# The start of a two-block transformer kernel: first weights loaded piece by piece between the halves of x, squares of x summed on GpSimd, rounded parts of two pieces ahead of the rests

## What is computed

```python
def rmsnorm(x, g):
    xf = x.astype(jnp.float32)
    y = xf * lax.rsqrt(jnp.mean(xf * xf, axis=-1, keepdims=True) + EPS)
    return (y * g.astype(jnp.float32)).astype(x.dtype)
...
        h = rmsnorm(x, g_mix[i])
        z = h @ w_in[i]                                   # 1024 x 2560
        b_gate, c_gate, x_in, u, v = jnp.split(z, splits, axis=-1)
        y_conv = short_conv_mixer(b_gate, c_gate, x_in, w_conv[i])
        y_sgu = sgu_mixer(jax.nn.gelu(u), jax.nn.gelu(v), g_sgu[i], w_spatial[i], b_spatial[i])
        x = x + jnp.concatenate([y_conv, y_sgu], axis=-1) @ w_out[i]
```

## Time and profile before

| | |
|---|---|
| time, median of 3 runs | 951.76 us (950.13 to 953.07) |
| the profiled execution's span | 949.0 us |
| median less that span | 2.76 us |
| TensorE busy | 921.4 us, 97% |
| TensorE weight loads (beside the products) | 650.6 us, 69% |
| VectorE / ScalarE / GpSimd busy | 501.4 / 330.9 / 36.0 us |
| read from HBM | 287.43 MB, 304 GB/s over the span |

### The profile page before, as it was taken

The page is one execution under the profiler, slowest core; times in us unless marked ns, Lnnn a source line. Parts: engine busy times, 40 slices in busy tenths (PEclk is TensorE's granted clock), DMA queues, the critical chain, the costliest instruction groups (busy, mean ns, idle before and its releaser), DMA issues.

```text
span 949.0 us, 14172 instructions
## 1 busy us (share of the span) xinstructions
PE 921.4 (97%) x5886; PEld 650.6 (69%) x5886; DVE 501.4 (53%) x867; ACT 330.9 (35%) x528; POOL 36.0 (4%) x39
## 2 busy tenths in 40 slices
PE   7999999999999899999999999999999999999997
PEld 6997734443444445334344389989999999999886
DVE  7784612221222312222222199999898977766642
ACT  6832210101011000001101088556566755644541
POOL 1000000000000000000000000123220000000000
PEclk9999999999999999999999999999999999999999
DMA  9997799999999999999999984643433435554301
GB/s 334 407 388 311 302 387 430 424 431 430 430 430 432 428 427 431 429 430 430 430 430 422 422 357 177 246 163 126 168 134 144 178 111 194 227 202 178 134 1 44
DMA packets 28981, 289.45 MB, mean 305 GB/s; under 512 B 3056, under 2 KB 6384, under 8 KB 12400
## 3 DMA queue, kind: packets, MB, share of 16 engines
q1 hardware_dynamic: 28192, 286.91, 74.0%
q10 hardware_dynamic: 720, 1.57, 0.4%
HBM read 287.43 MB, written 1.05 MB: 304 GB/s over the span
## 4 chain that ended last, share of the span: by engine, by line
PE 86%; DVE 8%; ACT 3%; issue 2%; DMA 0%; DVEq 0%; POOL 0%; ACTq 0%
PE ps L279 85%; DVE wl L275 3%; PE ps L1081 1%; ACT wh L268 1%; DMA arena<-in_xT 0%; ACT arena L1903 0%; DVE arena L393 0%; DVE arena L1944 0%; DVE arena L2015 0%; DVE ple_l L1477 0%; ACT h_h L1449 0%; DVE arena L1486 0%; DVE mg_l L1951 0%; ACT arena L1906 0%; DVE mix_l L624 0%
## 5 line engine op out<-in xcount | busy, mean ns | idle before, releaser
L279 PE MATMUL ps<-ring,arena 128*64 128x512 f32 x1216 | 340.2, 600 | 5.9 <-issue 5.9
L275 DVE TENSOR_TENSOR wl<-ring,wh 128x1024 fp32r<-128x1024 f32 x150 | 181.5, 1243 | 40.2 <-ACT wh L268 40.1
L279 PEld LDWEIGHTS ps<-ring,arena 128*64 128x64 f32 x1216 | 109.1, 138 | 125.0 <-issue 123.2
L268 ACT ACTIVATE wh<-ring 128x1024 fp32r<-128x1024 f32 x150 | 151.9, 1053 | 43.2 <-PE ps L279 30.4
L279 PE MATMUL ps<-arena 128*64 128x512 f32 (+4 forms) x448 | 158.4, 522 | 0.5 <-DVE arena L1173 0.3
L1186 DVE SCALAR_TENSOR_TENSOR arena<-ps,arena 128x512 f32<-128x512 f32 x16 | 12.0, 752 | 205.0 <-PE ps L279 205.0
L279 PEld LDWEIGHTS ps<-arena 128*64 128x64 f32 (+2 forms) x448 | 54.7, 144 | 86.6 <-issue 82.1
L279 PE MATMUL ps<-up_h,wh 128*128 128x256 f32 x352 | 85.7, 282 | 0.7 <-ACT up_h L2004 0.7
L279 PE MATMUL ps<-up_l,wh 128*128 128x256 f32 x352 | 82.3, 280 | 0.0
L1256 ACT ACTIVATE y_h<-ps 128x512 fp32r<-128x512 f32 x32 | 19.0, 597 | 151.7 <-PE ps L279 151.7
L279 PEld LDWEIGHTS ps<-up_h,wh 128*128 128x128 f32 x352 | 66.3, 188 | 0.9 <-issue 0.9
(11 more groups left out here) (279 smaller groups left out, 1466.3 us busy)
## 6 DMA issues: line engine op xcount, KB each, us to landing
ring<-in_moe SPq DMA_DIRECT2D x69, 2048.0 KB, 23.6
arena<-in_moe SPq DMA_DIRECT2D x17, 2048.0 KB, 23.6
ring<-in_w_in SPq DMA_DIRECT2D x12, 2048.0 KB, 9.7
ring<-in_w_up SPq DMA_DIRECT2D x11, 2048.0 KB, 7.6
ring<-in_moe SPq DMA_DIRECT2D x24, 512.0 KB, 15.3
ring<-in_w_dn SPq DMA_DIRECT2D x5, 2048.0 KB, 8.1
ring<-in_w_out SPq DMA_DIRECT2D x4, 2048.0 KB, 16.1
arena<-in_moe SPq DMA_DIRECT2D x8, 512.0 KB, 13.9
```

Source lines behind the costliest of these rows:

```text
L268: e.activation(wh(i), raw_piece(i), ACT.Copy).then_inc(*hi.up(i))
L275: e.tensor_tensor(wl(i), raw_piece(i), wh(i), SUB).then_inc(*lo.up(i))
L279: return e.matmul(o, l, r, start=first, stop=final, skip_group_check=True)
```

## The change

- The host lays the first load out by pieces, so that each piece is 4 KB in one stretch per partition, where it was eight stretches of 512 bytes.
- SyncE's order becomes: first half of x, gains, piece 0, second half of x, piece 1, pieces 2 and 3 together, and the rest as before.
- All eight squares are made by GpSimd, which then adds them up itself: chunks 4 to 7 onto 0 to 3 (128 x 1024 values), 2 and 3 onto 0 and 1 (512), 1 onto 0 (256). TensorE multiplies the one sum, after piece 2, where it multiplied eight squares ahead of piece 0.
- TensorE begins with seven float32 products of ones into an unused bank, which wait for nothing but memsets; then piece 0's products with x's rounded parts and rests for chunks 0 to 3 and for 4 to 7, then piece 1's, then the rests of pieces 0 and 1, piece 2, the sum's product, piece 3.
- ScalarE makes piece 0's rounded part between the halves of x, and pieces 1 to 5 before the root r1 (before: 0 to 3). VectorE makes the rests of pieces 0 to 5 before the reciprocal (before: 0 to 3).

```diff
@@ mixer_pe
-            squares((1, 0, 3, 2, 5, 7, 4, 6))
-            three(e, ps[3][:, 0:256], "in1", 0, 0, XGH, XGL, xg)
-            for j in range(1, 4):
-                three(e, ps[3 + j][:, 0:256], "in1", 0, j, XGH, XGL)
+            for x in range(7):
+                mm(e, ps[7][:, 0:256], inv1024, ones[:, 0:2, :].rearrange("p a b -> p (a b)"), x == 0, x == 6)
+            e.wait_ge(*hi.at(0))
+            products(0, range(4), wh, xg_h)
+            products(0, range(4), wh, xg)
+            products(0, range(4, 8), wh, xg_h)
+            products(0, range(4, 8), wh, xg)
+            e.wait_ge(*hi.at(1))
+            products(1, range(8), wh, xg_h)
+            products(1, range(8), wh, xg)
+            rounded_rest(0)
+            rounded_rest(1)
+            three(e, ps[5][:, 0:256], "in1", 0, 2, XGH, XGL)
+            e.wait_ge(*sum0.at("all"))
+            mm(e, ps[2][:, 0:256], inv1024, SQ0[:, 0, :], True, True).then_inc(*means.up("r1"))
+            three(e, ps[6][:, 0:256], "in1", 0, 3, XGH, XGL)
@@ mixer_dve
-                if c in (0, 2):
-                    e.tensor_tensor(SQ0[:, c, :], XT[:, c, :], XT[:, c, :], M).then_inc(*sq0_v.up(c))
-                    e.wait_ge(*sq0_v.at(c))
-                elif c in (4, 6):
-                    e.wait_ge(*sq0_a.at(c))
-                else:
-                    e.wait_ge(*sq0_p.at(c))
+                e.wait_ge(*sq0.at(c))
...
-            split_lo(e, 4)
+            split_lo(e, 6)
@@ mixer_act
             for c in range(8):
+                if c == 4:
+                    split_hi(e, 1)
...
-                if c in (4, 6):
-                    e.activation(SQ0[:, c, :], XT[:, c, :], ACT.Square).then_inc(*sq0_a.up(c))
-            split_hi(e, 4)
+            split_hi(e, 6)
@@ mixer_pool
-            for c in range(1, 8, 2):
+            for c in range(8):
                 e.wait_ge(l_xT if c < 4 else l_xT2, 16)
-                e.tensor_tensor(SQ0[:, c, :], XT[:, c, :], XT[:, c, :], M).then_inc(*sq0_p.up(c))
+                e.tensor_tensor(SQ0[:, c, :], XT[:, c, :], XT[:, c, :], M).then_inc(*sq0.up(c))
+            e.wait_ge(*sq0.at(7))
+            e.tensor_tensor(SQ0[:, 0:4, :], SQ0[:, 0:4, :], SQ0[:, 4:8, :], ADD).then_inc(*sum0.up("four"))
+            e.wait_ge(*sum0.at("four"))
+            e.tensor_tensor(SQ0[:, 0:2, :], SQ0[:, 0:2, :], SQ0[:, 2:4, :], ADD).then_inc(*sum0.up("two"))
+            e.wait_ge(*sum0.at("two"))
+            e.tensor_tensor(SQ0[:, 0, :], SQ0[:, 0, :], SQ0[:, 1, :], ADD).then_inc(*sum0.up("all"))
@@ loads
-            e.dma_start(XT[:, 4:8, :], dr["xT"][:, 4:8, :]).then_inc(l_xT2, 16)
...
-                    dst, src = (v.rearrange("p (c n) -> p c n", c=8) for v in (dst, src))
-                    e.dma_start(dst[:, :, 0:128], src[:, :, 0:128]).then_inc(ring_sem[k], 16)
-                    e.dma_start(dst[:, :, 128:256], src[:, :, 128:256]).then_inc(l_second, 16)
-                    e.dma_start(dst[:, :, 256:512], src[:, :, 256:512]).then_inc(s_half, 16)
+                    e.dma_start(dst[:, 0:1024], src[:, 0:1024]).then_inc(ring_sem[k], 16)
+                    e.dma_start(XT[:, 4:8, :], dr["xT"][:, 4:8, :]).then_inc(l_xT2, 16)
+                    e.dma_start(dst[:, 1024:2048], src[:, 1024:2048]).then_inc(l_second, 16)
+                    e.dma_start(dst[:, 2048:4096], src[:, 2048:4096]).then_inc(s_half, 16)
@@ _layout
+    r["w_in"][0] = r["w_in"][0].reshape(128, 8, 4, 128).transpose(0, 2, 1, 3).reshape(128, -1)
```

More of the change, by code:

```diff
@@ L216, in raw_piece @@
                 return w[:, j * 1024:j * 1024 + 1024]
-            if name == "pgate":
+            if name == "pgate" or (name, n) == ("in1", 0):
                 return piece_view(w[:, j * 1024:j * 1024 + 1024], name)
@@ L428, in build @@
         xg_h = sig("x_hi", range(8))
-        sq0_v, sq0_a, sq0_p = sig("sq0_v", [0, 2]), sig("squares", [4, 6]), sig("sq0_p", range(1, 8, 2))
+        sq0 = sig("sq0", range(8))
+        sum0 = sig("sum0", ["four", "two", "all"])
         xg = sig("x_lo", range(8))
@@ L475, in mixer_pe, with products, rounded_rest @@
         def mixer_pe(e):
-            def squares(cs):
+            def products(j, cs, v, ready=None):
                 for c in cs:
[L478 to L481, removed]
-            e.wait_ge(*made.at("ones"))
-            squares((1, 0, 3, 2, 5, 7, 4, 6))
-            three(e, ps[3][:, 0:256], "in1", 0, 0, XGH, XGL, xg)
-            for j in range(1, 4):
-                three(e, ps[3 + j][:, 0:256], "in1", 0, j, XGH, XGL)
+                    if ready is not None:
+                        e.wait_ge(*ready.at(c))
+                    k = mm(e, ps[3 + j][:, 0:256], v(j)[:, c, :], (XGL if ready is xg else XGH)[:, c, :],
+                           v is wh and ready is not xg and c == 0, v is wl and c == 7)
+                return k
+            def rounded_rest(j):
+                e.wait_ge(*lo.at(j))
+                products(j, range(8), wl).then_inc(*proj.up("in1", 0, j))
+            e.wait_ge(*made.at("ones"))
+            for x in range(7):
[14 more added lines that the diff above has]
+            three(e, ps[6][:, 0:256], "in1", 0, 3, XGH, XGL)
             for i in range(2):
@@ L651, in build @@
         xc = sig("xc", range(2))
-        vsq = sq0_a.then(range(2))
+        vsq = sig("squares", range(2))
         vvar = sig("vvar", [0])
```

## The result

The changed kernel takes 955.79 us (median of 5 runs, 954.78 to 957.18) against 951.02 us for the kernel before beside it: a ratio of 1.0055, 95% interval 1.0044 to 1.0067, so 5.2 us slower (4.2 to 6.4). The profiled execution took 956.97 us and has a span of 955.2 us, which leaves 1.8 us around the span.

What follows compares the result with a forecast made beforehand. TensorE was taken to bound the start, transfers from 138 to 328 us. Turns with GpSimd's additions (4.0 us) put piece 3's end at 26.4, half clock (0.6) at 27.0; 3.4 us late after VectorE's last rest: 951.76 + 3.4 = 955.2, range 950.9 to 956.8.

Steps and rivals of the forecast that it cites:

- a shift at the start reaches the end one for one: Each us TensorE wins or loses at 27 us counts as one us at the end, in either direction.
- second mark: Start of TensorE's first product with rests of pieces 4 to 7: forecast 30.75 against 27.35 before, 3.4 us late.
- x's second half at 9.5: In the first transfers, x's second half lands behind piece 0 at 9.5 us, 1.4 us later than before.
- Rival (d): The layout fails and x's second half comes at 10.5: one us more in every case, 956.2 us; chance 0.05.
- The pairs of square and rest: GpSimd's squares and VectorE's rests of x alternate: after square 4, three pairs of 0.82 us each, to 12.65.
- The long addition goes first: GpSimd's addition of 1024 columns runs ahead of VectorE's rest of chunk 7, from 12.65 to 14.9, 2.25 us.
- Who goes first: When both want to run, waiting GpSimd goes before the next VectorE operation; likely, with the other order kept as rival.
- (b): VectorE makes chunk 7's rest first, additions slip between pieces' rests: 0.9 to 2.1 us slower, 953.4 us; chance 0.22.
- (c): VectorE wins every meeting and TensorE waits for the late sum: 3.8 us slower with half clock, 955.6; chance 0.10.
- (a): VectorE and GpSimd don't hinder each other where it counts: 0.35 us faster, 951.4 us; chance 0.13.
- The clock: TensorE runs 3.3 us after 15.2 at half clock: 0.6 us lost after hiding by a wait, bounds 0 and 1.9.
- first mark: Start of TensorE's first product with 512 columns, where piece 3 ends: forecast 27.0 against 23.60 before.

Runs made afterwards that it cites:

- e10: Changed kernel without additions, squares on three engines as before, their products where TensorE waits for x, pieces 4 and 5 behind root and reciprocal: 949.51 us, ratio 0.9993.
- e3: Changed kernel with the rounded parts and rests of pieces 4 and 5 put back behind the root and the reciprocal: 957.28 us, ratio 1.0073.
- e8: Kernel before with the new layout of the first load and seven products of ones ahead of the squares' products, x's second half still ahead of piece 0: 949.61 us, ratio 0.9983.
- e2: Changed kernel with nine more products of ones, so that TensorE doesn't stand idle before 15.2 us: 953.8 us, ratio 1.0043.
- e1: Changed kernel with GpSimd's three additions left out, TensorE multiplying the square of chunk 0 alone: 952.59 us, ratio 1.0016.
- e4: Kernel before with only the new layout of the first load and the new order of its transfers: 952.26 us, ratio 1.0017.
- e7: Kernel before with only the seven products of ones put ahead of the squares' products: 949.72 us, ratio 0.9989.
- e6: Kernel before with GpSimd's squares and additions, seven products of ones and the one late product; transfers, layout and orders as before: 957.63 us, ratio 1.007.
- e5: Changed kernel with one more wait: GpSimd begins its additions only when the rest of x's chunk 7 is made: 953.16 us, ratio 1.0023.
- e9: e5 with five more products of ones to keep TensorE's clock up: 954.4 us, ratio 1.0037.

## Why the prediction was right

The forecast was 955.2 us and 3.4 us slower; measured are 955.79 and 5.2 slower (4.2 to 6.4). The direction and the mechanism were right, the size was too small. By its steps:

- **That a shift at the start reaches the end one for one**: right up to 300 us, and not contradicted behind. Read from the two traces product by product, counted back from the end, the delay is 4.1 us at the second mark, 4.4 at 54 us and still 4.4 at 128 and at 300 us. In all eleven traces of the changed kernel and the experiments the delay at 300 us is within 0.3 us of that at the second mark, from 1.3 us early (e10) to 8 us late (e3). Behind that single executions wander: here it is 4.6 at 530, 5.6 at 560, 6.5 at 650 and 6.2 at the end, with no edit in between. The stretch from 300 to 650 us grows by 2.2 us here, by 1.2 in e8, 0.8 in e2, 0.6 in e1 and in e4, and shrinks by 0.2 in e7, all against the same profile of before, so a part of it is that profile. The difference of the medians is 4.8 us: the profiled execution of the changed kernel took 1.2 us more than its median, and that of before, at 1.8 us over its span, 0.3 less than 951.02, which accounts for the rest of the 6.2.
- **x's second half at 9.5**: 9.68 here; over all profiles 9.8 against 8.3 (the means of the times above; 8.6 without e6's), 1.2 to 1.5 us later where I said 1.4. e4 measures what this alone costs: 1.6 us. Rival (d) had 10.5; three of the eight executions come near it or pass it (10.30, 10.46, 10.74), so it fell for this trace and not in general.
- **The pairs of square and rest**, 0.82 each to 12.65: the squares ended at 12.41, seven rests at 12.69.
- **The long addition goes first**: 12.48, ahead of the rest issued at 12.61. Its price was taken as 2.25 and is 2.41, the upper end of my bounds. The estimate from the Trainium skill's figure (GPSIMD Engine Reference, Performance versus the Vector engine) was 2.25 too, and this trace's 2.41 decides. Rest of chunk 7: 15.2 forecast, 15.18 measured; rest of piece 0: 17.5 and 17.40; rest of piece 1: 19.25 and 19.07.
- **Who goes first**: at the start GpSimd, waiting, never let a second VectorE operation past, and neither in e5, where it stood behind exactly one rest. It isn't a rule: the row at 639.40 comes again in the changed kernel at 645.97, where an addition of 256 columns took 2.02 us while VectorE, busy since 645.73, ran three more operations that were issued after it, at their usual length:

```profile
645.33 2.06 DVE L1596 SCALAR_TENSOR_TENSOR arena<-arena,vec 128x256 f32<-128x256 f32 x5
645.97 2.02 POOL L1860 TENSOR_TENSOR arena<-arena 128x256 f32<-128x256 f32 x1 [5.55 <-ACT arena L1605]
```

In the trace of before at least ten of the 30 operations of L1842 went first like this, more than the seven that the prediction names. What sets the order is open, so GpSimd's going first at the start was likely and not certain, as the prediction had it. The Trainium skill (SBUF — State Buffer, Summary: rules for kernel authors) has it that the second one to issue is blocked until the first is done. The six instructions at the start agree (2.57 us for an operation of 0.48); at 645.97 three that were issued later went first, and there the measurement decides. Rivals (b) and (c) fell at the start, (a) by e1 and e5.
- **The clock**: I had 3.3 us at half and 0.6 us for it, with 1.9 as the bound. It was 6.8 us, 4.5 of them in the products, and e2 puts 1.1 us on it, by its mark. This term was mis-sized by half a us. e1 and e3 show 3.4 and 10 us of it, with the same products in the same order up to the mean.
- **The second mark**: 30.75 forecast, 31.48 measured. Of the 0.73, 0.37 is there at the first mark already (27.37 for 27.0), where the clock is the term that was too small. The other part is a turn that I hadn't seen:

```profile
28.33 1.92 POOL L785 TENSOR_SCALAR_AFFINE_SELECT arena<-arena 128x1024 f32<-128x1024 f32 x1 [10.35 <-DMA arena<-in_wsT]
29.22 0.42 DVE L593 TENSOR_TENSOR arena<-ps,arena 128x256 f32<-128x256 f32 x1
29.55 1.78 DVE L275 TENSOR_TENSOR wl<-ring,wh 128x1024 fp32r<-128x1024 f32 x1
```

GpSimd's mask comes when its transfer lands, at 28.3; before, VectorE's last rest was long done by 25.1, now it meets the mask, and takes 1.78 instead of 1.2. The profile counts 0.22 us of TensorE's time as the wait for it; its sixteen products of 512 columns start 0.233 us apart from 27.37, which would be 31.10 for the next, and it starts at 31.48. This price is read from one execution. The operation at 29.22, which has one operand in PSUM (`ps`), takes its usual 0.42 beside the mask: it doesn't take turns.

One step of the working was loose: the 2.76 us between the median and the profiled span. It is 1.8 us in the changed kernel (956.97 less 955.2), so the profiled execution of before was 1 us under the median of three, 951.76, that the forecast was added to. As only differences were added to that median, the 3.4 isn't touched, but the 955.2 is: beside the changed kernel the one before measured 951.02, 0.74 us less. That 955.2 and 955.79 lie so close is in part luck; with the later median the same forecast would have been 954.4.

So 3.4 us stand against 5.2, 0.8 under the lower end of the interval. The traces place 0.7 of the missing 1.8 before the second mark (the clock and the mask's turn) and 0.3 between it and 54 us, for which no cause was looked for. The remaining 0.3 to 0.8 (with the difference of the medians, 4.8, or the ratio, 5.2) isn't placed. Two small slips of the working change nothing: 10.15 and three times 0.82 make 12.61 and not 12.65, and the 1.05 us that hide half clock are the waits for the rests of pieces 0 and 1 together (0.3 and 0.8).

## What to carry to other kernels

An engine that seems idle isn't free if it shares an entrance to memory with a busy one: GpSimd had nothing else to do here, and its 4 us of additions cost 3.7 us at the end (3.0 by the marks), because VectorE's operations with two SBUF operands had to take turns with them; an operation with one operand in PSUM that met GpSimd's mask didn't (29.22). The instruction that pays is the one that stands behind the longest turn, so first look which of the neighbour's instructions the critical engine waits for: one more wait, which put the additions behind it, gave 3.0 us back (2.2 by the marks). And fillers that keep TensorE's clock up were worth something here where TensorE itself was the bound (e7 by the medians, e2 by its mark alone), and nothing beside a wait that hid the half clock anyway (e9).

## What was unexpected of the hardware

- TensorE's first products ran at half speed for 3.5 to 6 us, differently long in each execution (the half-products of ones and of squares start 0.43 us apart and then 0.21), while the column for the granted clock has 1.00 there.
- The granted clock fell to 0.50 after TensorE had been busy from 1.5 to 7.0 us and then with gaps, none longer than 1.1 us, and stayed there for 6.8 us, 4.5 of them with products back to back; in e3 it stayed for 10 us. One begins at 12.9, in e1 at 12.5, in e5 at 10.9; which products it meets differs from one execution to the next.
- The time at which the second half of x lands behind piece 0 differs by up to 1.9 us: 8.84 to 10.74 over eight kernels which issue their first transfers in the same order, one execution of each. It is as large as most of the effects looked for here.
